# Shifting the split activations of an fp32r transformer trunk by 128 to 384 bytes against the weights in SBUF

## The chip, the cores and the metric

One core of one Trainium2 chip runs the whole program in one launch. The metric is the device time of the launch in microseconds (us). The kernel before takes 1123.65 us (median of 3 runs, 1123.19 to 1123.92).

## The reference

A two-layer streaming encoder trunk on 512 tokens of width 1024, all in float32. Layer 0 mixes tokens with sliding-window attention (16 heads, 4 key/value heads, a learned sink per head, a relative-position bias); layer 1 with gated linear attention in chunks of 64. Each mixer is followed by a gated feed-forward block of width 2816, with a causal convolution of width 3 on the gate branch. What matters here is the dense products:

```python
def conv_ffn(h, w_up, conv_w, conv_b, w_down):
    u = h @ w_up
    gate, up = u[..., :D_FF], u[..., D_FF:]
    ...
    return (jax.nn.silu(conv) * up) @ w_down

def reference(x, ...):
    for i in range(DEPTH):
        h = rmsnorm(x, mix_norm[i])
        y = swa_sink_attention(...) if i % 2 == 0 else gla(...)
        x = x + y
        x = x + conv_ffn(rmsnorm(x, ffn_norm[i]), ...)
    return rmsnorm(x, final_norm)
```

## The kernel before, in words

**Layout.** Activations are kept transposed: 128 features on the partitions, 512 tokens along them, so an activation tile is 128x512 float32, 2048 bytes in each partition. A tensor of 1024 features has 8 such tiles (X, XH, XL, OH, OL, YH, YL), one of 2816 has 22 (AH, AL).

**Split products.** Each float32 operand of a dense product is split into a high part that is rounded to fp32r and a low part that is the remainder: XH and XL for the normalized input, OH and OL for attention's output, YH and YL for that of the gated linear attention, AH and AL for the feed-forward activation, WH and WL for the weights. A product is three fp32r matmuls for each block of 128 input features, into one PSUM bank: WH with the high activation, WH with the low one, WL with the high one (`product`, line 305, its matmul on line 315). Each matmul of this loop has a stationary operand of 128x128 (a weight block, 512 bytes in each partition) and a moving operand of 128x512 (an activation tile), and each loads its stationary operand anew: a LDWEIGHTS (PEld in the profile) that runs beside the matmul before it.

**Units.** The weights come in 172 units of 128 output features: 8 blocks (1024 columns) in each unit, 11 (1408 columns) in those of the down projections, where two units make one output tile. Units go through four slots: SP loads one into WRAW[slot], ACT rounds it into WH[slot] (`hi`, line 678, and the loops on lines 743 to 762), DVE subtracts into WL[slot], which lies on WRAW (`lo`, line 1006), and TensorE takes it (`unit`, line 320). Semaphores order all of this; nothing is planned at run time. Two units have buffers of their own (FIFTH_*).

**Order of TensorE's work.** Attention's projections with XH and XL, mixed with the attention's small matmuls; the output projection with OH and OL; the up projection of 44 units with XH and XL (a hardware loop on line 340); the down projection of 16 units with AH and AL (line 371; line 362 is one unit written apart); then the same for layer 1, with YH and YL. The very last output tile is computed in two halves of 256 tokens (`last_tile`, line 636).

**Placement, the part that the diff touches.** `place` (line 77) lays tensors one behind the other in SBUF by hand. A float32 tensor starts at the next multiple of 64 bytes. A tensor of type fp32r (line 80) is first moved up to the next address whose remainder modulo ROW = 512 is PHASE = 128:

```python
            if at is None and dt == F32R:
                place_at[0] += (PHASE - place_at[0]) % ROW
```

The weight slots are 4*11*128 = 5632 bytes apart, eleven times 512, blocks within a slot 512 bytes, activation tiles 2048. So every weight block and every activation tile of a split product starts at remainder 128. WRAW, FIFTH_RAW and GA are put at remainder 128 by lines of their own. Three sets of tensors (feed-forward, attention, gated linear attention) share the SBUF behind `region` (line 127). The float32 tensors that follow a split one take what remainder comes: GS, CV and AC behind AL (lines 132 to 134) begin at 128, 192 and 192, the attention's KT to PT at 64. GT and GK (lines 169, 170) lie on the place of YH and YL before these are written.

The tiny matmuls between the units are float32, not fp32r: two matmul records each, at 128 or 256 columns (lines 415, 433, 550, 566, 579, 581), and transposes (395, 423, 522, 558).

Of the kernel before, what the change touches and what calls it, by code (L numbers as in the profile page):

```python
# [51 lines left out]
TH = T // 2  # L52
DVE_TILES = 6
ROW, PHASE = 512, 128


A_K, A_V, A_Q, A_O = 0, 2, 4, 12
# [14 lines left out]
def trunk(nc, xT, gains, w_qkv, sinks, rel_bias, w_o, w_bin, w_ga, w_gate, b_norm, w_bo, w_up, conv_w, conv_b,  # L72
          w_down, onehot, ident, causal, causal_pair, out, bias_rows):
    with ExitStack() as ctx:
        place_at = [-(-nc.sbuf_base // 64) * 64]

        def place(name, shape, dt=F32, at=None):

            size = 4 * int(np.prod(shape[1:]))
            if at is None and dt == F32R:  # L80
                place_at[0] += (PHASE - place_at[0]) % ROW
            offset = place_at[0] if at is None else at
            if at is None:
                place_at[0] += -(-size // 64) * 64
            return nc.alloc_sbuf_tensor_at(name, shape, dt, offset=offset)
# [3 lines left out]


        X = place("X", [P, KT_D, T])
        XH = place("XH", [P, KT_D, T], F32R)
        XL = place("XL", [P, KT_D, T], F32R)
        WH = place("WH", [P, SLOTS, HALF * P], F32R)
        slots_at = place_at[0] + (PHASE - place_at[0]) % ROW
# [34 lines left out]
        AH = place("AH", [P, FT, T], F32R)  # L130
        AL = place("AL", [P, FT, T], F32R)
# [18 lines left out]
        OH = place("OH", [P, KT_D, T], F32R)  # L150
        OL = place("OL", [P, KT_D, T], F32R)
# [11 lines left out]
        VV = place("VV", [P, 4, BH * HV])  # L163
        S = place("S", [P, NCH // 2, HV])
        SG = place("SG", [P, KT_D, T])
        y_at = place_at[0] + (PHASE - place_at[0]) % ROW
        YH = place("YH", [P, KT_D, T], F32R)
        YL = place("YL", [P, KT_D, T], F32R)
        GT = place("GT", [P, 4, 2, T], at=y_at)
# [1342 lines left out]
```

## Time and profile before

| | us |
|---|---|
| median of 3 runs | 1123.65 |
| the profiled execution, its own time | 1123.7 |
| its span, first to last instruction | 1121.9 |
| PE busy (matmul) | 1099.9, 98% |
| PEld busy (weight loads, beside the matmuls) | 906.0, 81% |
| DVE busy | 577.8, 52% |
| ACT busy | 484.8, 43% |
| POOL busy | 160.8, 14% |
| mean granted TensorE clock, share of 2.4 GHz | 0.997 |

A matmul's record covers it from its issue to its modelled end, and successive records overlap, so a matmul with 389 ns in the profile doesn't hold the engine for 389 ns. What one costs is the distance from its start to the next one's start; where they run without a gap, that is a stretch of the chain divided by its count.

### The profile page before, as it was taken

Reading aid. Unit: us, or ns where it says so; the run is one execution under the profiler, and the core shown is the slowest. Engines: PE = TensorE matmul, PEld = TensorE weight load, DVE = VectorE, ACT = ScalarE, POOL = GpSimd, SP = SyncE. Lnnn points to the kernel's source line nnn. Section 1 sums busy time; section 2 is a strip of 40 time slices with the busy share of each in tenths; the row PEclk is TensorE's granted clock in tenths of the full one; section 3 lists DMA queues with packets and bytes.
Section 4 is the critical chain, followed back from the end, with each engine's and each line's share of the span. In section 5 each row is a group of like instructions: output and inputs, shape, how many; then the busy total and the mean of one; then the engine's idle time right before and its main releaser. Section 6 shows DMA issues by size and latency. Waiting matters only on the chain.

```text
span 1121.9 us, 14060 instructions
## 1 busy us (share of the span) xinstructions
PE 1099.9 (98%) x5162; PEld 906.0 (81%) x5162; DVE 577.8 (52%) x734; ACT 484.8 (43%) x707; POOL 160.8 (14%) x123
## 2 busy tenths in 40 slices
PE   6999999999999999999999999999999999999996
PEld 5888778888888888888788888778888888888886
DVE  4588565555555553334354556866455555542214
ACT  6366555444454432222652345454544544431211
POOL 6100021111111110001021221121111111110001
PEclk9999999999999999999999999999999999999998
DMA  6511122222222232221222211222222223332212
GB/s 193 160 65 60 36 99 93 100 100 99 93 93 93 101 128 81 100 96 57 79 87 94 80 43 59 84 96 94 93 93 93 93 98 106 108 104 104 84 71 76
DMA packets 31622, 103.48 MB, mean 92 GB/s; under 512 B 3873, under 2 KB 8641, under 8 KB 31586
## 3 DMA queue, kind: packets, MB, share of 16 engines
q1 hardware_dynamic: 27680, 100.68, 26.2%
q10 hardware_dynamic: 3906, 2.31, 1.1%
q8 instruction: 24, 0.39, 0.1%
q14 instruction: 12, 0.10, 0.0%
HBM read 99.56 MB, written 2.88 MB: 91 GB/s over the span
## 4 chain that ended last, share of the span: by engine, by line
PE 89%; DVE 5%; ACT 3%; DMA 1%; POOL 1%; issue 1%; SPq 0%; DVEq 0%; POOLq 0%
PE PS L315 78%; DVE WL L1006 2%; PE PS L636 1%; PE PS L362 1%; PE PS L415 1%; POOL SS L1350 1%; ACT WH L678 1%; PE PS L433 1%; DVE X L1031 1%; ACT SQ L708 1%; PE PS L423 1%; DMA X<-xT 1%; PE PS L547 1%; PE PS L579 0%; PE PS L566 0%
## 5 line engine op out<-in xcount | busy, mean ns | idle before, releaser
L315 PE MATMUL PS<-XH,WH 128*128 128x512 f32 x992 | 393.9, 397 | 9.9 <-DVE XL L1024 9.8
L315 PE MATMUL PS<-XH,WL 128*128 128x512 f32 x992 | 387.2, 390 | 0.0
L315 PE MATMUL PS<-XL,WH 128*128 128x512 f32 x992 | 386.9, 390 | 0.0
L1006 DVE TENSOR_TENSOR WL<-WRAW,WH 128x1024 fp32r<-128x1024 f32 (+1 forms) x169 | 228.9, 1355 | 242.5 <-ACT WH L747 72.0
L315 PEld LDWEIGHTS PS<-XH,WH 128*128 128x128 f32 x992 | 186.7, 188 | 53.5 <-issue 11.8
L315 PEld LDWEIGHTS PS<-XH,WL 128*128 128x128 f32 x992 | 186.6, 188 | 39.6
L315 PEld LDWEIGHTS PS<-XL,WH 128*128 128x128 f32 x992 | 186.8, 188 | 39.2 <-issue 1.7
L1360 POOL TENSOR_TENSOR CV<-CV,R 128x512 f32<-128x512 f32 x44 | 70.5, 1603 | 416.7 <-ACT CV L724 416.7
L315 PE MATMUL PS<-AH,WH 128*128 128x512 f32 x308 | 119.8, 389 | 0.0
L315 PE MATMUL PS<-AL,WH 128*128 128x512 f32 x308 | 119.8, 389 | 0.0
L315 PE MATMUL PS<-AH,WL 128*128 128x512 f32 x308 | 119.8, 389 | 0.0
L678 ACT CAST WH<-WRAW 128x1024 fp32r<-128x1024 f32 (+1 forms) x65 | 70.4, 1083 | 86.1 <-DMA WRAW<-w_bin 56.4
L747 ACT CAST WH<-WRAW 128x1024 fp32r<-128x1024 f32 x40 | 42.0, 1051 | 106.2 <-DMA WRAW<-w_up 106.2
L1350 POOL TENSOR_TENSOR SS<-SS,SQ 128x512 f32<-128x512 f32 x34 | 47.1, 1386 | 222.3 <-ACT SQ L708 219.6
L727 ACT CAST AH<-AC 128x512 f32 (+1 forms) x44 | 27.3, 620 | 114.8 <-DVE AC L1057 114.8
L1057 DVE TENSOR_TENSOR AC<-PS,CV 128x512 f32<-128x512 f32 x44 | 30.4, 692 | 73.1 <-POOL CV L1360 73.1
L315 PEld LDWEIGHTS PS<-AL,WH 128*128 128x128 f32 x308 | 57.8, 188 | 12.1
L315 PEld LDWEIGHTS PS<-AH,WL 128*128 128x128 f32 x308 | 57.8, 188 | 12.0
L315 PEld LDWEIGHTS PS<-AH,WH 128*128 128x128 f32 x308 | 57.8, 188 | 11.9
L1059 DVE TENSOR_TENSOR AL<-AC,AH 128x512 f32 (+1 forms) x44 | 30.5, 693 | 39.4 <-ACT AH L727 39.4
L758 ACT CAST WH<-WRAW 128x1408 fp32r<-128x1408 f32 x12 | 16.5, 1374 | 64.4 <-DMA WRAW<-w_down 64.4
L707 ACT ACTIVATE XH<-X,GAIN 128x512 fp32r<-128x512 f32 (+1 forms) x24 | 17.4, 724 | 60.9 <-DVE X L1031 60.9
(204 smaller groups left out, 1206.3 us busy)
## 6 DMA issues: line engine op xcount, KB each, us to landing
WRAW<-w_up SPq DMA_DIRECT2D x88, 512.0 KB, 3.2
WRAW<-w_down SPq DMA_DIRECT2D x32, 704.0 KB, 4.0
WRAW<-w_bin SPq DMA_DIRECT2D x24, 512.0 KB, 3.2
WRAW<-w_qkv SPq DMA_DIRECT2D x11, 512.0 KB, 4.7
WRAW<-w_o SPq DMA_DIRECT2D x7, 512.0 KB, 3.6
WRAW<-w_bo SPq DMA_DIRECT2D x7, 512.0 KB, 3.3
X<-xT SPq DMA_DIRECT2D x4, 512.0 KB, 6.7
out<-X SPq DMA_DIRECT2D x5, 256.0 KB, 2.2
```

Of the source, the lines that this page charges most:

```text
L315: last = mm(PS[:, bank], w[:, c:c + P], x[:, kb], start=start and n == 0 and w is wh and x is hi, stop=stop and n == len(kbs) - 1 and w is wl)
L362: last = mm(PS[:, 0], w[:, 1, n * P:(n + 1) * P], x[:, kb], start=False, stop=n == HALF - 1 and w is WL)
L678: nc.scalar.copy(WH[:, s, 0:k * P], WRAW[:, s, 0:k * P]).then_inc(hi_ready, 1)
L707: A(XH[:, tile, :], X[:, tile, :], ACT.Copy, scale=GAIN[:, st, tile]).then_inc(xh_ready, 1)
L727: nc.scalar.copy(AH[:, tile, :], AC[:, par:par + 1, :]).then_inc(ah_ready, 1)
L747: nc.scalar.copy(WH[:, s + 1, 0:D], WRAW[:, s + 1, 0:D]).then_inc(hi_ready, 1)
L758: nc.scalar.copy(WH[:, s], WRAW[:, s]).then_inc(hi_ready, 1)
L1006: tt(WL[:, s, 0:k * P], WRAW[:, s, 0:k * P], WH[:, s, 0:k * P].bitcast(F32), ALU.subtract)\
L1057: tt(AC[:, par], PS[:, up], CV[:, par], ALU.mult).then_inc(unit_evac, 1)
L1059: tt(AL[:, tile, :], AC[:, par:par + 1, :], AH[:, tile, :].bitcast(F32), ALU.subtract).then_inc(al_ready, 1)
L1350: nc.gpsimd.tensor_tensor(SS[:], SS[:], SQ[:, par], ALU.add).then_inc(ss_ready, 1)
L1360: nc.gpsimd.tensor_tensor(CV[:, j], CV[:, j], R[:], ALU.mult).then_inc(slr_ready, 1)
```

## The change

A table gives, for eight split activations, how many bytes past remainder 128 they are placed; `place` and the hand-made address of YH add it. Weights and all others have no entry and stay at 128. The remainders modulo 512 become: XH and XL 256, AH 320, AL 448, OH 448, OL 320, YH 0, YL 256.

```diff
@@ -52,6 +52,7 @@
 ROW, PHASE = 512, 128
+BEHIND = {"XH": 128, "XL": 128, "AH": 192, "AL": 320, "OH": 320, "OL": 192, "YH": 384, "YL": 128}
@@ -78,7 +79,7 @@
             size = 4 * int(np.prod(shape[1:]))
             if at is None and dt == F32R:
-                place_at[0] += (PHASE - place_at[0]) % ROW
+                place_at[0] += (PHASE + BEHIND.get(name, 0) - place_at[0]) % ROW
             offset = place_at[0] if at is None else at
@@ -163,7 +164,7 @@
         SG = place("SG", [P, KT_D, T])
-        y_at = place_at[0] + (PHASE - place_at[0]) % ROW
+        y_at = place_at[0] + (PHASE + BEHIND["YH"] - place_at[0]) % ROW
         YH = place("YH", [P, KT_D, T], F32R)
```

## Rows read from the trace of the kernel before

**Rows 1.** The page: busy time of PE, and the chain that ended last.
```profile
PE 1099.9 (98%) x5162; PEld 906.0 (81%) x5162; DVE 577.8 (52%) x734; ACT 484.8 (43%) x707; POOL 160.8 (14%) x123
...
PE 89%; DVE 5%; ACT 3%; DMA 1%; POOL 1%; issue 1%; SPq 0%; DVEq 0%; POOLq 0%
```

**Rows 2.** Chain of waits, windows 200:240 and 1093:1104: start us, us, what.
```profile
199.83 40.35 PE PS L315 x178
...
1093.79 9.71 PE PS L636 x81
```

**Rows 3.** Window 200:500: busy us of each engine, clock, DMA share, GB/s.
```profile
200.00:500.00 300.00, 300.00 (x1325) 248.40 (x1324) 143.44 (x160) 124.72 (x139) 39.98 (x26) 1.00 0.29 98
```

**Rows 4.** Waits in window 200:400: us in total, times, longest us.
```profile
POOL CV L1360 <- ACT CV L724: 178.2, 19, 10.6
ACT WH L747 <- DMA WRAW<-w_up: 47.5, 18, 2.9
```

**Rows 5.** Groups by shape on PE: count, busy us, mean ns, idle us before.
```profile
L315 PE MATMUL PS<-XH,WH 128*128 128x512 f32 x992 | 393.9, 397 | 9.9 <-DVE XL L1024 9.8
L315 PE MATMUL PS<-XH,WL 128*128 128x512 f32 x992 | 387.2, 390 | 0.0
L315 PE MATMUL PS<-XL,WH 128*128 128x512 f32 x992 | 386.9, 390 | 0.0
L315 PE MATMUL PS<-AH,WH 128*128 128x512 f32 x308 | 119.8, 389 | 0.0
...
L315 PE MATMUL PS<-OH,WH 128*128 128x512 f32 x56 | 22.7, 405 | 0.0
L315 PE MATMUL PS<-YH,WH 128*128 128x512 f32 x56 | 22.3, 398 | 0.0
...
L636 PE MATMUL PS<-AH,WH 128*128 128x256 f32 x44 | 12.6, 286 | 0.0
...
L362 PE MATMUL PS<-AH,WH 128*128 128x512 f32 x22 | 8.6, 389 | 0.0
...
L315 PE MATMUL PS<-OH,FIFTH_HI_A 128*128 128x512 f32 x8 | 3.1, 389 | 0.0
...
L489 PE MATMUL PS<-XH,GA 128*128 128x512 f32 x8 | 3.1, 389 | 0.0
```

**Rows 6.** Timeline, the first matmuls of the program: start us, us, what.
```profile
8.54 0.63 PE L315 MATMUL PS<-XL,WH 128*128 128x512 f32 x1
...
11.53 0.62 PE L315 MATMUL PS<-XH,WL 128*128 128x512 f32 x1
```

**Rows 7.** Line 566, float32 matmuls: timeline, and min/median/max ns of one.
```profile
636.80 1.46 PE L566 MATMUL PS<-VV,KUT 128*128 128x256 f32 x6
...
L566 PE MATMUL PS<-VV,KUT x24: 377/378/379, 636.8 to 696.1; 128*128 128x256 f32 x24
```

**Rows 8.** Timeline, split matmuls just behind the small ones of line 522.
```profile
567.47 0.40 PE L315 MATMUL PS<-XL,WH 128*128 128x512 f32 x1
...
569.79 0.39 PE L315 MATMUL PS<-XH,WL 128*128 128x512 f32 x1
...
571.83 0.39 PE L315 MATMUL PS<-XH,WL 128*128 128x512 f32 x1
```

**Rows 9.** Line 315, windows 567.2:570 and 200:500: min/median/max ns of one.
```profile
L315 PE MATMUL PS<-XL,WH x4: 387/389/396, 567.5 to 569.6; 128*128 128x512 f32 x4
L315 PE MATMUL PS<-XH,WL x4: 389/394/397, 567.7 to 569.8; 128*128 128x512 f32 x4
...
L315 PE MATMUL PS<-XL,WH x298: 389/389/389, 199.7 to 401.6; 128*128 128x512 f32 x149
```

**Rows 10.** Groups by shape on DVE: count, busy us, mean ns, idle us before.
```profile
L1059 DVE TENSOR_TENSOR AL<-AC,AH 128x512 f32 x40 | 27.7, 692 | 36.6 <-ACT AH L727 36.6
...
L1161 DVE TENSOR_TENSOR PB<-PB,RD 128x512 f32<-128x512 f32 x16 | 11.1, 692 | 0.6
```

## The prediction

> **What bounds the kernel now.** I read the page first: PE is busy 98% of the span and the chain that ended last is 89% PE [rows 1]. Then the chain itself: in the hardware loops it is one piece of matmuls of line 315 with no other engine in it, 178 of them in 40.35 us, so 226.7 ns from start to start [rows 2]. Then the reserve of the others: between 200 and 500 us DVE is busy 143 of 300 us, ACT 125, the DMA engines 29% of the time [rows 3], and nobody is waited for by PE there; the waits are those of POOL for ACT and of ACT for a DMA [rows 4]. So the time is the number of split matmuls times their spacing.
>
> The number, from the groups by shape [rows 5]: 3 x 992 with XH or XL; 3 x 308 on line 315 and 3 x 22 on line 362 with AH or AL; 3 x 56 each for O and Y; 3 x 8 each with the FIFTH buffers (the group of A stands for that of B); 2 x 8 with GA. That is 2976 + 990 + 168 + 168 + 48 + 16 = 4366 matmuls of 512 columns, and 132 of 256 columns on line 636. 4366 x 226.7 ns = 990 us, 88% of the span.
>
> **How much of a spacing is not columns.** 512 columns at 2.4 GHz are 213.3 ns; 226.7 measured leaves 13.4. The 256-column matmuls of line 636 start every 9.71 / 81 = 119.9 ns [rows 2], against 106.7 ns of columns: 13.2 left. So the surplus is a fixed amount for each matmul with its weight load, not a share of the columns. Two rows show it absent. The program's first matmuls, with the same tensors at the same addresses, start 2.99 us / 7 = 427.1 ns apart [rows 6]; that is 512 columns at 1.2 GHz (426.7) and 0.4 ns more. The page's slice for that stretch doesn't show the lower clock, so I take the level from the spacing. And the float32 matmuls of line 566, whose 256 columns pass at half rate (213.3 ns), start (1.46 - 0.378) / 5 = 216.4 ns apart [rows 7]: 3.1 ns over. So the surplus comes only where the moving operand is read at full rate, 4 bytes of a partition in 1/2.4 ns, while the next weight block is read too. 13.3 ns is what 32 columns take, and 32 columns are 128 bytes of the tile. Weight block and tile begin at the same remainder, and the load's record begins with the matmul's. A stall for as long as both reads sit in the same 128 bytes of the 512 would give just this number. That is a reading, not shown: no row of before has two different distances.
>
> A third observation says that the relative position in time matters, at the least. Behind the small matmuls of line 522 the split matmuls don't run at 226.7: from 567.47 to 569.79 us ten of them take 2.32 us, 232.0 each, and the next nine 2.04 us, 226.7 again [rows 8]. The records of the first ten last 387 to 397 ns, where all 298 of a group in the loops last 389 [rows 9]. So the stream falls, after some ten matmuls, into a fixed relation between its two reads, and on the way it passes relations that cost more and one that costs 2 ns less.
>
> **The change, term by term.** All the moves but one go together, since they have one answer: (a) Instructions: none is added, removed or reordered, no wait, no DMA; the queues are as before. (b) ACT and DVE write XH, XL and the rest at other remainders, and GS, CV and AC come 320 bytes further round. DVE's subtraction into AL from AC (remainder 192) and its product on PB (remainder 64) both take 692 ns for 512 elements [rows 10], so I cost it at 0. It is hidden under PE anyway, but for the last 11 us behind the last matmul, where X, R and STD keep their remainders, and some short waits of the stage borders. (c) Padding: at most some hundred bytes in each region; no transfer changes its size. (d) The weights stay at remainder 128, since `place` moves each of them up to it again.
>
> (e) The spacing of the 4498 split matmuls. Nothing in the trace prices it at another distance, so it is bounded. From below: the surplus falls to that of line 566, 13.4 - 3.1 = 10.3 ns saved on 4366 and 13.2 - 3.1 = 10.1 ns on 132, in sum 46 us. From above: the stream never finds the good relation and runs at 232.0 throughout, 5.3 ns x 4366 = 23 us more. Between them lies the nearest row, the same instruction with the same operands in another relation, with a record of 387 ns in place of 389 [rows 9]: 2 ns x 4498 = 9.0 us saved. I take this one: a shift of the tile against the block is, to the memory, much like a shift in time, and the row shows that there is a cheaper relation than that of the loops, though not that a stream can stay in it. The sum: 1123.7 for the profiled execution less 9.0 is 1114.7; against the median of 1123.65, from which the execution differs by 0.05, it is 1114.6 us.
>
> As to rules: the trace has 3.1 ns of surplus as the least at the full clock [rows 7]. The Trainium skill, TensorE: Matmul & The Clock Gate, section Back-to-back issue gap, gives the isolated gap at full clock as the columns plus 2.5 ns, 215.8 ns for 512; by that 10.9 ns x 4498 = 49 us could go, an estimate that ends at 1075 us. No row shows such a spacing for fp32r.
>
> **The rivals.** *The whole stall goes (0.21).* If it is there only because both reads begin in the same 128 bytes, every tensor of the table leaves it: all distances are 128 to 384 of 512, at least 128 either way. Then the spacing is near 216.4 and the time 1123.7 - 46 = 1077.3 us. For it: the surplus is one quantity for 512 and 256 columns, is 128 bytes' worth, and is absent at half rate. Against it: the tile is read twice as fast as the block, so it gains 512 bytes on it during the 106.7 ns of a load and crosses its remainder once, wherever both began. Shifted, the crossing falls in the middle of the load.
>
> *No change (0.20).* The surplus is a cost of changing the stationary operand, 32 cycles of the array, or the memory is divided finer than 64 bytes or by partition only, so that no shift by a multiple of 64 is seen. For it: 544 cycles for 512 columns and 288 for 256 are round numbers, steady to the record. Against it: the stretch behind line 522 [rows 8], where the same pair costs 5.3 ns more for a while. Time 1123.7 us. The Trainium skill, SBUF — State Buffer, section SBUF: two separate sides, says that within the engine side PE never waits on anyone, and the TensorE page, section Step-by-step: what each phase is for, that loading the next weights takes no read bandwidth from the running matmul, since each has its own port. By these rules an address can't matter and the time is that of this rival; the first matmuls [rows 6] fit them, the 232.0 ns of the unsettled stretch [rows 8] speak against them.
>
> *Slower (0.26).* Equal remainders are the good case, and the relation into which the loops fall exists only there. The mechanism: the tile's read runs ahead of the load from the first column, and the two meet only when the load ends. Shifted by 128 to 384 bytes, the read overtakes the load while it is under way, and both are in the same 128 bytes for longer. Its place is every matmul of line 315, and it decides as soon as the stall of an overtaking in mid-load is longer than 13.4 ns. Its price is that of the unsettled stretch, 5.3 ns x 4366 = 23 us: 1146.8 us. For it: of the unsettled records only the shortest is below that of the loops [rows 9]. Against it: that stretch too is at equal remainders, so the distance isn't what made it dear.
>
> That the change doesn't do what it says can be left out: the padding is arithmetic, and every one of the eight names goes through the line that adds it. What could happen is that it does it for some tensors only. XH and XL carry 68% of the matmuls, AH and AL 25%.
>
> **How the numbers follow.** The forecast, a spacing that is shorter by some ns but not free of the stall, has 0.33 and a range of its own of 1097 (6 ns saved) to 1121 us. With the 0.21 of the whole stall gone it makes 0.54 for faster by more than 0.2%, which is about what a measurement of this kernel can tell from no change; 0.20 for within it; 0.26 for slower. The range begins at 1075, just under the whole stall gone (the spacing of line 566 is known to 2 ns only), and has to take in no change; above, it reaches 1137 us, three ns for each matmul, which leaves out the upper half of the slower case, some 0.13, and below a few in a hundred. So it is wide, because one unknown per matmul is multiplied by 4498.
>
> **What would show it.** In the profile after, the chain between 200 and 240 us again one piece of line 315, its time divided by its count below 226.7: 224.7 by the forecast, 216.4 if the stall is gone, 226.7 for no change, 232 for slower. The stretches with A (from 402 us on), O and Y have other distances than that with X; if the distance is what counts, their spacings may differ from one another, and if it is only equal or unequal, they will be alike. Line 636 keeps its 256 columns and should lose the same ns as line 315. The first matmuls should stay at 427 ns, lines 415 to 581 unchanged, DVE's and ACT's means the same to a ns or two. I am wrong if the spacing is unchanged and the time moves, or if DVE's or ACT's instructions change their length.

## The result, and the profile after

The changed kernel takes 1143.78 us (median of 4 runs, 1142.98 to 1143.98) against 1123.79 us of the kernel before on the same chip: the ratio is 1.0178, with a 95% interval of 1.016 to 1.0195. It is 20 us slower. I had forecast 1114.6 us with a range up to 1137, and both are wrong; the rival "slower", at 1146.8 us, comes within some 3 us.

The page of the profile after; every line number has moved by one, 315 to 316:

```profile
span 1141.2 us, 14060 instructions
...
PE 1121.0 (98%) x5162; PEld 908.5 (80%) x5162; DVE 578.1 (51%) x734; ACT 484.8 (42%) x707; POOL 160.9 (14%) x123
...
PE 89%; DVE 4%; ACT 3%; DMA 1%; POOL 1%; issue 1%; SPq 0%; DVEq 0%; POOLq 0%
...
L316 PE MATMUL PS<-XH,WH 128*128 128x512 f32 x992 | 398.8, 402 | 8.5 <-DVE XL L1025 8.5
L316 PE MATMUL PS<-XH,WL 128*128 128x512 f32 x992 | 392.1, 395 | 0.0
L316 PE MATMUL PS<-XL,WH 128*128 128x512 f32 x992 | 392.0, 395 | 0.0
...
L316 PE MATMUL PS<-AH,WL 128*128 128x512 f32 x308 | 121.6, 395 | 0.0
L316 PE MATMUL PS<-AH,WH 128*128 128x512 f32 x308 | 121.0, 393 | 0.0
L316 PE MATMUL PS<-AL,WH 128*128 128x512 f32 x308 | 120.3, 391 | 0.0
```

The mean granted clock is 0.996, as good as the 0.997 of before. The instructions are the same in number, the chain is still 89% PE, and DVE, ACT and POOL are busy as long as before to 0.3 us [rows 1]. The records of the split matmuls have become longer, by 5 ns on average with X, by 2 to 6 ns with A [rows 5]. Records overlap, so what that costs is read from the starts: added up from each matmul's start to the next one's over the whole trace, those with X take 13.1 us more than before, with A 4.4, with Y 0.9, with O 0.5, and those of 256 columns 0.3 less. That is 18.7 of the 19.3 us by which the span has grown. So nearly all of it lies in the split matmuls, and it isn't one place but a few ns on each.

The chain of waits of the kernel after, in windows 300:400, 430:500 and 1090:1120 (start us, us, what), answers to [rows 2]:

```profile
299.93 100.16 PE PS L316 x431
...
429.95 70.26 PE PS L316 x304
...
1112.85 7.18 PE PS L637 x61
```

As before, each stretch is one piece of matmuls with no other engine in it. With X they start 232.4 ns apart (100.16 / 431), with A 231.1, where both were at 226.7; the 256-column ones of the last tile are at 117.7 ns, where they were at 119.9. The records themselves are no longer alike. Line 316 in window 300:400 of the kernel after, with minimum, median and maximum ns:

```profile
L316 PE MATMUL PS<-XL,WH x144: 390/393/404, 299.8 to 399.5; 128*128 128x512 f32 x144
L316 PE MATMUL PS<-XH,WL x144: 390/393/405, 300.0 to 399.7; 128*128 128x512 f32 x144
...
L316 PE MATMUL PS<-XH,WH x144: 390/393/404, 300.2 to 399.9; 128*128 128x512 f32 x144
```

Before, all 298 of such a group lasted 389 [rows 9]. By the starts in the trace the spacings with X now go round in a cycle of seven matmuls, 241, 232, 231, 232, 228, 230, 233 ns, with A in one of nine between 226 and 236. The hardware loops don't come to rest at one spacing but run through several, over and over. In the stretch of layer 0 with X, 1031 matmuls on end, each spacing behind the first 15 is within 1 ns of the one seven matmuls before it. DVE, ACT and the DMA engines, which write the weight slots, work now and rest then: between 200 and 500 us they are busy 140 of 300 us, 123 and 28% of the time. So the other engines' writes don't make the loss: it lies in TensorE's own stream.

At the lower clock the distance costs nothing. The first matmuls of the kernel after, at start us, us, what:

```profile
8.72 0.63 PE L316 MATMUL PS<-XL,WH 128*128 128x512 f32 x1
...
11.71 0.63 PE L316 MATMUL PS<-XH,WL 128*128 128x512 f32 x1
```

Seven spacings in 2.99 us are 427.1 ns each, the same as before [rows 6]; by the spacing that is 1.2 GHz. The first spacings of the runs below are 426 to 427 ns too, with X at 0, 32, 64, 128 and 320.

What should not have changed did not. DVE's two instructions of [rows 10] in the kernel after:

```profile
L1060 DVE TENSOR_TENSOR AL<-AC,AH 128x512 f32 x40 | 27.7, 693 | 36.6 <-ACT AH L728 36.6
...
L1162 DVE TENSOR_TENSOR PB<-PB,RD 128x512 f32<-128x512 f32 x16 | 11.1, 692 | 0.5
```

### The profile page after: what moved, and what is told of

Read it like the earlier page. It is cut to its first block, busy times and chain, and to the rows that moved or that the text cites. A ratio compares the mean times of both kernels' runs of the same rounds, so it can differ in the third digit from the quotient of the medians.

```text
span 1141.2 us, 14060 instructions
## 1 busy us (share of the span) xinstructions
PE 1121.0 (98%) x5162; PEld 908.5 (80%) x5162; DVE 578.1 (51%) x734; ACT 484.8 (42%) x707; POOL 160.9 (14%) x123
## 4 chain that ended last, share of the span: by engine, by line
PE 89%; DVE 4%; ACT 3%; DMA 1%; POOL 1%; issue 1%; SPq 0%; DVEq 0%; POOLq 0%
PE PS L316 80%; DVE WL L1007 2%; PE PS L637 1%; PE PS L363 1%; PE PS L416 1%; POOL SS L1351 1%; ACT WH L679 1%; PE PS L434 1%; DVE X L1032 1%; ACT SQ L709 1%; PE PS L424 1%; DMA X<-xT 1%; PE PS L548 1%; PE PS L580 0%; PE PS L567 0%
## 5 line engine op out<-in xcount | busy, mean ns | idle before, releaser
L316 PE MATMUL PS<-XH,WH 128*128 128x512 f32 x992 | 398.8, 402 | 8.5 <-DVE XL L1025 8.5
L316 PE MATMUL PS<-XH,WL 128*128 128x512 f32 x992 | 392.1, 395 | 0.0
L316 PE MATMUL PS<-XL,WH 128*128 128x512 f32 x992 | 392.0, 395 | 0.0
L316 PEld LDWEIGHTS PS<-AH,WL 128*128 128x128 f32 x308 | 57.8, 188 | 13.4
```

What stands on the lines that cost most here:

```text
L316: last = mm(PS[:, bank], w[:, c:c + P], x[:, kb], start=start and n == 0 and w is wh and x is hi, stop=stop and n == len(kbs) - 1 and w is wl)
```

## The experiments

Spacings that are given without a chain line are worked out from the starts in the trace, over the longest unbroken stretch of a tensor's matmuls, the first 15 left out, in whole cycles. A cycle is the number of matmuls after which the spacings repeat. Distance is the remainder of the tile less that of the weights, for the high and the low part. The edits are shown against the changed kernel, that of `cols` against the kernel before, and only their main lines; where a name can be missing from the table, the address of YH takes 0 for it.

**Is it the place or the distance?** Two kernels. `together` moves everything that is split to remainder 256:

```diff
-ROW, PHASE = 512, 128
-BEHIND = {"XH": 128, "XL": 128, "AH": 192, "AL": 320, "OH": 320, "OL": 192, "YH": 384, "YL": 128}
+ROW, PHASE = 512, 256
+BEHIND = {}
```

> All split tensors, weights and activations alike, start at remainder 256 instead of 128; no distance between them. If only the distance between tile and weight block counts, the loops settle at 226.7 ns from matmul to matmul and the time is that of before, 1123.8 us. If an activation's own remainder counts (128 good, others bad), the spacing is above 230 ns and the time near 1144 us.

Measured: 1123.8 us against 1124.44 of before, ratio 0.9999 (0.999 to 1.0009). Chain in window 300:400 of `together`:

```profile
299.77 100.41 PE PS L316 x443
```

226.7 ns. `weights_back` is the reverse: the activations have remainder 128, as in the kernel before, and the weights have moved to 0.

```diff
-ROW, PHASE = 512, 128
-BEHIND = {"XH": 128, "XL": 128, "AH": 192, "AL": 320, "OH": 320, "OL": 192, "YH": 384, "YL": 128}
+ROW, PHASE = 512, 0
+BEHIND = {"XH": 128, "XL": 128, "AH": 128, "AL": 128, "OH": 128, "OL": 128, "YH": 128, "YL": 128}
```

> Weights (and GA, the FIFTH buffers) at remainder 0, all split activations at 128, where they are before the change. The distance is 128 everywhere. If the distance counts, all stretches run at 232.4 ns as X did with its own shift of 128, and the time is near 1144 us. If the activations' own place counts, they run at 226.7 ns and the time is 1124 us.

Measured: 1144.55 us (one run; before 1124.66). Chain in windows 300:400 and 430:500 of `weights_back`:

```profile
299.97 100.16 PE PS L316 x431
...
429.87 70.18 PE PS L316 x302
```

Both at 232.4 ns, as X at its distance of 128 in the changed kernel. So the remainder of a tensor by itself costs nothing, and the distance between tile and weight block costs all of it. One stretch differed from what was expected: Y settled at 233.3 ns, in a cycle of two (229, 238).

**Do the groups add up?** `x_only` moves XH and XL alone, `x_back` all but these:

```diff
-BEHIND = {"XH": 128, "XL": 128, "AH": 192, "AL": 320, "OH": 320, "OL": 192, "YH": 384, "YL": 128}
+BEHIND = {"XH": 128, "XL": 128}
```
```diff
-BEHIND = {"XH": 128, "XL": 128, "AH": 192, "AL": 320, "OH": 320, "OL": 192, "YH": 384, "YL": 128}
+BEHIND = {"AH": 192, "AL": 320, "OH": 320, "OL": 192, "YH": 384, "YL": 128}
```

> Only XH and XL are moved, by 128. If each group of matmuls is slowed by its own distance alone, the stretches with X run at 232.4 ns as after the change, those with AH and AL at 226.7 ns as before, and the time is 1123.8 us and some 2345 settled matmuls x 5.7 ns = 13.4 us, so 1137 us. If another tensor's new place (GS, CV, AC behind AL) costs the time, this run is near 1124 us.

> The changed kernel with XH and XL back at the weights' remainder; AH, AL, OH, OL, YH, YL stay moved. If the groups add up, X runs at 226.7 ns again and what is left is 958 settled A matmuls x 4.4 ns = 4.2 us, O 0.4 and Y 0.9, less 0.3 for the 132 matmuls of 256 columns: 5.2 us over before, 1129 us. If the whole loss hung on something that all share, it stays near 1144.

Measured: `x_only` 1139.66 us against 1124.44, ratio 1.0136 (1.0119 to 1.0153); `x_back` 1128.19 against 1123.83, ratio 1.0037 (1.0022 to 1.0052). 1.36% and 0.37% make 1.73%, where the change as a whole made 1.78%. The rest of each kernel was untouched: A ran at 226.7 ns in the first, X in the second. GS, CV and AC, which of these two kernels move in `x_back` only, cost nothing that is seen.

`x_only` lost 15.3 us (1.36% of 1123.8) where 13.4 were expected, and its chain says where a part of it is. Windows 300:400, the up projection of layer 0, and 800:900, that of layer 1:

```profile
299.93 100.16 PE PS L316 x431
...
799.81 100.33 PE PS L316 x430
```

232.4 ns in the first, 233.3 in the second, 1.0 us over a thousand matmuls: the same loop, the same tensors, the same addresses. In the changed kernel the second ran at 232.4 like the first. So at a distance of 128 there are two cycles, and whichever a stretch falls into holds it for a thousand matmuls on end. The addresses don't decide between them; that it is the way in which a stretch is entered is likely but not shown. Y shows the same: its distances are the same in `x_back` and in the changed kernel, and it settled at 233.3 in the one and 232.4 in the other.

**The whole circle of distances.** Three kernels with high and low part of a tensor at one distance, three or four distances in each kernel (the table of the changed kernel, which these lines replace, is left out, and the comments are added here):

```diff
+BEHIND = {"XH": 64, "XL": 64, "AH": 128, "AL": 128, "OH": 192, "OL": 192, "YH": 256, "YL": 256}    # scan1
+BEHIND = {"XH": 320, "XL": 320, "AH": 384, "AL": 384, "OH": 448, "OL": 448, "YH": 320, "YL": 320}  # scan2
+BEHIND = {"XH": 32, "XL": 32, "AH": 224, "AL": 224, "OH": 96, "OL": 96, "YH": 160, "YL": 160}      # scan3
```

> Distances, high and low part alike: X 64, A 128, O 192, Y 256. If the distance alone counts, A runs at 128 as X did after the change, 232.4 ns. If every unequal pair is alike, all four lie between 230 and 233. If the stall goes where the tile starts at least 128 bytes from the block, O and Y would be near 216 ns (which the changed kernel speaks against).

> Distances, high and low part alike: X 320, A 384, O 448, Y 320. If any unequal pair is bad, all four lie between 229 and 236 ns and the time is near 1144 us. If there is a distance that is better than equal remainders, its stretch lies below 226.7 ns.

> Distances between the 64-byte steps, high and low alike: X 32, A 224, O 96, Y 160. The steps of 64 gave 226.7, 228.9, 232.4 and 233.3 ns at 0, 64, 128 and 192 modulo 256. If the curve is smooth, 32 gives about 228, 96 about 231, 160 about 233, 224 about 230. If equal remainders are a special point, 32 and 224 are no better than 64 and 192. A stretch below 226.7 ns would be a better place than before's.

Measured: 1135.33, 1135.04 and 1148.31 us (one run each; before 1124.44 beside the first two, 1124.66 beside the third). The spacings:

| distance, bytes | spacing, ns | cycle, matmuls | from |
|---|---|---|---|
| 0 | 226.7 | 1 | before, together |
| 32 | 233.3 | 4 | scan3 X |
| 64 | 228.9 | 3 | scan1 X |
| 96 | 233.3 | 3 | scan3 O |
| 128 | 232.4 or 233.3 | 7 or 2 | scan1 A, weights_back Y |
| 160 | 234.3 | 7 | scan3 Y |
| 192 | 233.3 | 2 | scan1 O |
| 224 | 233.3 | 2 | scan3 A |
| 256 | 226.7 | 1 | scan1 Y |
| 320 | 228.9 | 3 | scan2 X, scan2 Y |
| 384 | 232.4 | 7 | scan2 A |
| 448 | 233.3 | 2 | scan2 O |

Some of the stretches themselves. `scan1`, chain in window 300:400 (X at 64) and timeline near 725 us (Y at 256):

```profile
299.89 100.25 PE PS L316 x438
```

```profile
724.65 0.39 PE L316 MATMUL PS<-YH,WH 128*128 128x512 f32 x1
...
730.99 0.39 PE L316 MATMUL PS<-YL,WH 128*128 128x512 f32 x1
```

228.9 ns, and 28 spacings in 6.34 us, which is 226.4 as read to 0.01 us and 226.7 by the starts. `scan2` in window 300:400 (X at 320) and `scan3` (X at 32, then A at 224):

```profile
299.78 100.25 PE PS L316 x438
```
```profile
299.83 100.33 PE PS L316 x430
...
429.80 70.23 PE PS L316 x301
```

Three things follow. The circle is 256 bytes, not the 512 of the kernel's ROW: 256 is as good as 0, and 320, 384 and 448 repeat 64, 128 and 192 to 0.1 ns and to the length of the cycle. Of the distances tried equal remainders are the best, and nothing lies below. And it is no smooth curve: 32 bytes off is as dear as 96 or 224, and 64 is the second best. My smooth guess for 32, about 228 ns, was 5 ns off. The table of the change had all four of its groups at places between 230.4 and 232.4.

The second state isn't peculiar to 128. `scan2` has one stretch with X at 320, window 533:542, that runs at 233.3 ns, where all its other stretches with X settle at 228.9; chain, and records of window 535:542:

```profile
532.94 9.10 PE PS L316 x39
```
```profile
L316 PE MATMUL PS<-XH,WH x11: 397/397/398, 534.6 to 541.6; 128*128 128x512 f32 x11
```

All its records last 397 or 398 ns, so one length of record alone doesn't mean the good state. At equal remainders no such second state was seen: each settled stretch of 512 columns, in every kernel that has one, is at 226.7.

**High and low part at different distances.** `mix1`, `mix2` and `mix3`, shown in the same way:

```diff
+BEHIND = {"XL": 64, "AH": 64, "OL": 128, "YH": 128}                                                # mix1
+BEHIND = {"XL": 192, "AH": 192, "OH": 64, "OL": 128, "YH": 128, "YL": 64}                          # mix2
+BEHIND = {"XH": 128, "XL": 192, "AH": 192, "AL": 128, "OH": 32, "OL": 32}                          # mix3
```

> High and low part at unequal distances, one of them 0: X (0, 64), A (64, 0), O (0, 128), Y (128, 0). If each matmul pays for its own tile alone, one third of the matmuls read the low tile: X = 226.7 + 2.2/3 = 227.4 ns, A = 228.2, O = 228.6, Y = 230.5. If the steps couple from one matmul to the next, the means come out otherwise, with a period over several matmuls; below 226.7 would be a gain over before.

> X (0, 192), A (192, 0), O (64, 128), Y (128, 64). By own tile alone: X = 226.7 + 6.6/3 = 228.9 ns, A = 231.1, O = (2 x 228.9 + 232.4)/3 = 230.1, Y = 231.2. The changed kernel's A (192, 64 modulo 256) would be 231.8 by this and measured 231.1.

> X (128, 192), A (192, 128), O (32, 32), Y (0, 0): the last pairs of the steps of 64. Every pair with a distance so far settled between 228.9 and 234.5 ns; these two should too, O at 233.3 as X did at 32, Y at 226.7. A value below 226.7 would be a better place.

Measured: 1144.22, 1137.38 and 1139.17 us, one run each. `mix1` (high, low): X (0, 64) 232.0, A (64, 0) 233.3, O (0, 128) 231.1, Y (128, 0) 228.9 ns. `mix2`: X (0, 192) 228.9, A (192, 0) 234.4, O (64, 128) 232.2, Y (128, 64) 232.2. `mix3`: X (128, 192) 231.1, A (192, 128) 231.1, O at 32 233.3, Y at 0 226.7. The sum by parts fails; of the eight it gave only X of `mix2` comes out as expected. One matmul in three off by 64 costs 5.3 ns on all three (0.7 expected), while two in three off by 128 cost 2.2 (3.8 expected). The chain of `mix1` in window 300:400 and its records:

```profile
299.82 100.22 PE PS L316 x432
```
```profile
L316 PE MATMUL PS<-XL,WH x145: 388/395/398, 299.7 to 399.9; 128*128 128x512 f32 x145
L316 PE MATMUL PS<-XH,WL x144: 390/393/402, 299.9 to 399.4; 128*128 128x512 f32 x144
```

XH stands at distance 0 here, and its matmuls with WL still last 390 to 402 ns. The addresses repeat, modulo 256, every three matmuls, and the spacings of this stretch only every fifteen. So what one matmul costs isn't given by its own addresses; it depends on the ones before it too. With these and the changed kernel all 16 pairs in steps of 64 (modulo 256) have been seen, and none is below (0, 0).

**Which pair counts?** `wl_shift` moves the low weights alone, and lets A, O and Y follow in different ways:

```diff
+BEHIND = {"AL": 448, "OL": 448, "YH": 448, "YL": 448}
-        slots_at = place_at[0] + (PHASE - place_at[0]) % ROW
+        slots_at = place_at[0] + (PHASE - 64 - place_at[0]) % ROW
```

> The low weights (and WRAW under them) start at remainder 64, the high ones at 128; XH, XL, AH, OH at 128; AL and OL at 64; YH and YL at 64. In the trace the load beside a matmul of a high tile reads WH, that beside one of a low tile reads WL. If the pair that counts is tile and the block loaded beside it, A and O have distance 0 in both pairs, though their tensors stand at two remainders, and run at 226.7 ns; X has (0, 64) and runs at 232.0 ns with mix1's period of 15; Y has (192, 0) and runs at 234.5 ns as mix2's A. If the pair that counts is tile and its own block, A has distances of 64 and 192 and isn't at 226.7. If all must stand at one remainder, none is.

Measured: 1141.58 us (one run; before 1123.83). A ran at 233.3 ns (cycle of 3), O in the same cycle, X at 231.1 (a cycle of 12 in the loop of layer 0, of 3 in that of layer 1) where 232.0 was expected, Y at 231.1 (3) where 234.5 was. The 24 matmuls of O with the FIFTH buffers, whose weights all stay at 128, have distances (0, 192) and ran at 228.9, as X of `mix2`. Chain in windows 300:400 and 430:500 of `wl_shift`:

```profile
299.82 100.30 PE PS L316 x434
...
429.89 70.23 PE PS L316 x301
```

A and O, apart from those 24, had distance 0 to the block that the trace shows being loaded beside each of their matmuls, and it didn't help. So the pair "tile and the block loaded beside it" alone doesn't decide. "Tile and its own block" fits, but isn't established by that: X then has one matmul in three off by 64, as X of `mix1` has, and ran in another cycle, which decides little, since one set of addresses can hold two. As far as these runs go, the good relation needs all four tensors, high and low tile, high and low weights, at one remainder; for the weights against each other that rests on this one kernel and its 64 bytes. It would let each read go on from one matmul to the next at the place in the circle where the last one ended; that reason is argued, not shown.

**Is the surplus a fixed cost of the weight change?** The surplus is the spacing less the time of the columns at 2.4 GHz. `cols` is the kernel before with fewer columns in some of the split products. It leaves out the last tokens there, so its output isn't whole, and it serves for spacings only. One of the edited calls is shown; the others pass 496, 488 and 508:

```diff
-                        last = mm(PS[:, bank], w[:, c:c + P], x[:, kb],
+                        last = mm(PS[:, bank, 0:cols], w[:, c:c + P], x[:, kb, 0:cols],
...
-                        unit(i + (u0 + s), s, XH, XL)
+                        unit(i + (u0 + s), s, XH, XL, cols=504)
```

> The kernel before, all at remainder 128, with the last tokens left out of the split products: 504 columns in the up projections' loops, 496 in the down projections, 488 in three of the last O units and 508 in three of the last Y units (their last 8, 16, 24 and 4 columns of the output hold old values). A stall of fixed length (13.3 ns for each matmul with its load) gives 504: 223.3, 496: 220.0, 488: 216.7, 508: 225.0 ns from start to start. If instead at equal remainders a start falls on a grid of 13.33 ns (226.7 = 17 steps, 120.0 = 9 steps) and a matmul needs its columns and some 2 to 3 ns more, then 504, 496 and 488 all run at 213.3 ns (16 steps) and 508 at 226.7 (17 steps), more than its columns would ask.

Measured: 1121.14 us (one run; before 1124.94). The chain in windows 300:400 (504 columns) and 430:500 (496), and the records of the first:

```profile
299.81 100.41 PE PS L315 x443
...
429.96 70.13 PE PS L315 x314
```
```profile
L315 PE MATMUL PS<-XL,WH x148: 388/388/388, 299.6 to 399.6; 128*128 128x504 f32 x148
```

504 columns run at 226.7 ns, as 512 do, so eight columns (3.3 ns) bring nothing. 496 run at 223.3, 488 at 225.7 (a cycle of seven, 221 to 242), 508 at 227.6. A fixed surplus of 13.3 ns would give 223.3, 220.0, 216.7 and 225.0, and is refuted: 488 columns take longer than 496, and the surplus goes from 13.3 ns at 512 columns to 22.4 at 488. My grid of 13.33 ns, which gives 213.3 for three of them, is refuted as well. Of the five counts 512 has the smallest surplus; it is the one whose read of a tile ends where the next begins, modulo 256 bytes. That this is the reason isn't shown.

No experiment points to a version that beats the kernel before. Only the 256-column matmuls are quicker at some unequal distances, in the changed kernel by 2.2 ns on 132 of them, 0.3 us in all.

## Why the prediction was wrong, point by point

- **What bounds the kernel, the count, the share of the surplus.** Right. The time is the number of split matmuls times their spacing, and 18.7 of the 19.3 us came in by the spacing; X with 68% of the matmuls brought 13.1 of them.
- **Terms (a) to (d), at nothing.** Right: DVE's instructions keep their 692 ns to 1 ns, and the placement of the float32 tensors behind AL in `x_back` costs nothing seen.
- **Term (e), the spacing.** This is the step that failed, and its sign with it. I took the single record of 387 ns as the nearest row, because "a shift of the tile against the block is, to the memory, much like a shift in time", and so put 2 ns saved on each matmul where the settled stretches lost 5.7 ns with X and 4.4 with A. That likeness isn't refuted as a picture: the single spacings of the unsettled stretch are 224 to 236 ns by the starts, those of the changed kernel 226 to 241. What failed is the step from one cheap matmul to a whole stream, which the text itself had said the row doesn't show. In the changed kernel there are cheap ones too, 226 ns twice in each cycle of nine with A, and each is followed by 230 to 236. The row that came close was the mean of 232.0 ns over the ten unsettled matmuls [rows 8], which I had used only as the upper bound and as a rival's price: X settled at 232.4, A at 231.1. Over the 15 unequal pairs in steps of 64 bytes the settled spacing averages 231.4 and runs from 228.9 to 234.4, so the mean was the better estimate, and that it hit X to 0.4 ns is in part luck.
- **The rival "slower".** It had the price (5.3 ns; 5.7 with X and 4.4 with A measured), though it put it on all 4366 matmuls, and those that were unsettled before lost next to nothing; and it had the right core, that equal remainders are the good case and that the state of the loops exists only there. Its mechanism, a read that overtakes the load in mid-load, isn't shown. It makes a large distance the cause, yet 32 bytes are as dear as 96 or 224.
- **The rival "the whole stall goes".** Refuted: no stretch of 512 columns came below 226.7 ns at any distance tried. The 128 bytes' worth of columns was a coincidence of numbers: the circle is 256 bytes, and at 504 or 488 columns the surplus is 16.7 or 22.4 ns.
- **The rival "no change".** Refuted for the fixed cost by `cols`, for an address that doesn't matter by `weights_back`. By SBUF — State Buffer of the Trainium skill, section SBUF: two separate sides, PE never waits on anyone. What I drew from the rules quoted there, that an address can't matter, is refuted: the address of one of PE's operands against the other is worth 1.8% of the kernel. Whether one of its reads waits for the other is not seen in a trace.
- **What should show it.** The last tile's 256-column matmuls were to move with the others. They went the other way, from 119.9 to 117.7 ns, so what a distance costs depends on the length of the matmul too. The first matmuls stayed at 427.1 ns, as said.
- **The range.** Its upper end stood at three ns for each matmul, little more than half of the slower case's own price. A case with a chance of 0.26 was cut where it was likeliest to land.

## What to carry to other kernels

Where fp32r matmuls of 512 columns stream with a new weight block each, place the moving tiles and the weight blocks at the same remainder modulo 256 bytes, the high and the low parts of a split product among them. All strides between tiles and between blocks were multiples of 256 here; others weren't tried. Judge it by the settled spacing, a stretch of the chain divided by its count. The records give a hint: a spread of 390 to 405 ns where they could all be 389 is a bad sign, but records of one length aren't a good one unless it is the short length. When an unknown relation has to be priced, take the mean over the unsettled stretch of the trace, not its best record; one case shows that here.

## What the runs showed of the hardware that I had not expected

The stream of split matmuls is very regular and has a memory over several matmuls. It settles into cycles of 1 to 15, most often the same to a ns from one stretch to another, but some sets of addresses hold two of them, at distance 128 with 232.4 and 233.3 ns, and a whole hardware loop keeps the one it falls into. At 1.2 GHz none of this is seen. The lengths of the cycles are round: 7 x 232.38 = 1626.7 ns, 9 x 231.11 = 2080.0, 3 x 228.89 = 686.7, 4 x 233.33 = 933.3 and 6 x 117.78 = 706.7 are within 0.1 ns multiples of 6.67 ns, the time of 16 columns or 64 bytes of a tile at 2.4 GHz. No run says why, and what in the memory has the period of 256 bytes stays open too. It wasn't tried to take the weight load away from beside a matmul, so that the two reads collide at all is inferred from their distance mattering, not seen.
